# Attention heads two at a time, and the recurrence output with tokens on partitions

## The reference

```python
o_intra = jnp.einsum('bnhts,bnshv->bnthv', att, v)          # inside a chunk
o_inter = jnp.einsum('bnthk,nbhkv->bnthv', q * jnp.exp(cum), s_start)   # state at the chunk's start
o = o_f + rev(o_b)                                          # both directions
o = rms_norm(o, onorm) * jax.nn.silu(hd(zg))                # mean square over a head's 64 channels
```

```python
s_loc = jnp.einsum('bnqhgd,bnkhd->bnhgqk', qb, kb) * SCALE   # masked to the window
s_ctx = jnp.einsum('bnqhgd,blhd->bnhgql', qb, kc) * SCALE
p = jax.nn.softmax(jnp.concatenate([s_loc, s_ctx, s_sink], axis=-1), axis=-1)
o = p[..., :nk] @ v_band + p[..., nk:] @ v_cache
merged = g_a * (y_a @ wb_a) + g_b * (y_b @ wb_b) + g_c * (y_c @ wb_c) + g_d * (y_d @ wb_d)
```

## Time and profile before

| | us |
|---|---|
| median of 3 runs (1871.96 to 1878.03) | 1876.58 |
| the profiled execution | 1872.46 |
| its span | 1870.6 |
| PE busy in the span | 1696.6 |
| DVE, ACT, POOL busy | 553.6, 416.7, 222.5 |

### The profile page before, as it was taken

The page is one execution under the profiler, slowest core; times in us unless marked ns, Lnnn a source line. Parts: engine busy times, 40 slices in busy tenths (PEclk is TensorE's granted clock), DMA queues, the critical chain, the costliest instruction groups (busy, mean ns, idle before and its releaser), DMA issues. The chain is left out here.

```text
span 1870.6 us, 26968 instructions
## 1 busy us (share of the span) xinstructions
PE 1696.6 (91%) x9388; PEld 1072.3 (57%) x9388; DVE 553.6 (30%) x1317; ACT 416.7 (22%) x869; POOL 222.5 (12%) x182
## 2 busy tenths in 40 slices
PE   6989999999999897899789899999999998878887
PEld 3656556665585554555466546566557755545455
DVE  2155563321115111111132465534111241111112
ACT  3121225530103111111122012355201211111110
POOL 0003020000000232232100030100000012232220
PEclk8998899999998999999999898999999989999998
DMA  9502126533227799999982022262323179999993
GB/s 364 203 23 76 30 87 210 178 119 106 75 91 268 281 373 387 355 374 392 362 293 80 23 90 34 69 229 70 118 90 135 68 256 335 389 379 354 374 383 129
DMA packets 166115, 385.93 MB, mean 206 GB/s; under 512 B 21020, under 2 KB 58908, under 8 KB 165536
## 3 DMA queue, kind: packets, MB, share of 16 engines
q1 hardware_dynamic: 140976, 340.28, 49.1%
q0 software_dynamic: 16992, 24.96, 5.7%
q10 hardware_dynamic: 8016, 18.97, 2.7%
HBM read 372.34 MB, written 31.98 MB: 216 GB/s over the span
## 5 line engine op out<-in xcount | busy, mean ns | idle before, releaser
L756 PE MATMUL ab<-hT,slot 128*128 128x384 f32 x1344 | 457.3, 497 | 13.4 <-PEq L765 7.2
L756 PE MATMUL vb<-slot,arena 128*64 128x256 f32 x2560 | 309.0, 396 | 74.3 <-PEq L806 74.3
L756 PEld LDWEIGHTS ab<-hT,slot 128*128 128x128 f32 x1344 | 258.9, 194 | 192.4 <-issue 26.5
L756 PEld LDWEIGHTS vb<-slot,arena 128*64 128x64 f32 x2560 | 206.4, 142 | 158.9 <-issue 97.7
L756 PE MATMUL vb<-arena 64*64 64x16 f32 (+3 forms) x1272 | 152.3, 345 | 27.7 <-PEq L765 24.4
L658 POOL DMA_INDIRECT expert_sums<-arena,sum_index x72 | 112.9, 1568 | 371.7 <-POOLq L647 173.8
L1982 DVE SCALAR_TENSOR_TENSOR arena<-vb,unit_gate,arena 128x128 f32<-128x128 f32 x80 | 28.1, 351 | 411.5 <-DVEq L1981 411.5
L756 PEld LDWEIGHTS vb<-arena 64*64 64x64 f32 (+2 forms) x1272 | 84.2, 180 | 70.6 <-issue 68.0
L756 PE MATMUL ab<-slot,hT 128*128 128x384 f32 (+1 forms) x384 | 118.8, 464 | 0.0
L790 PEld LDWEIGHTS ab<-con,arena 128*128 128x128 f32 x560 | 61.3, 142 | 87.3 <-issue 86.2
L1461 ACT ACTIVATE arena<-vb 128x128 f32<-128x128 f32 x92 | 25.5, 278 | 368.0 <-ACTq L1460 368.0
(11 more groups left out here) (257 smaller groups left out, 1601.7 us busy)
## 6 DMA issues: line engine op xcount, KB each, us to landing
slot<-in_w_up SPq DMA_DIRECT2D x64, 2048.0 KB
slot<-in_w_mod SPq DMA_DIRECT2D x24, 2048.0 KB
slot<-in_w_mgate SPq DMA_DIRECT2D x32, 1024.0 KB
nat<-in_w_down SPq DMA_DIRECT2D x32, 1024.0 KB, 19.5
slot<-in_w_in SPq DMA_DIRECT2D x10, 2048.0 KB
arena<-in_w_down SPq DMA_DIRECT2D x16, 1024.0 KB, 18.9
hT<-in_w_down SPq DMA_DIRECT2D x16, 1024.0 KB, 17.1
slot<-in_w_out SPq DMA_DIRECT2D x4, 2048.0 KB
```

The costliest lines, as they stand in the source:

```text
L756: i = nc.tensor.matmul(out, lhsT, rhs, start=start, stop=stop, skip_group_check=True)
```

## The change

**The recurrence output** has tokens on partitions now. Per block, four products have all 128 rows and 128 columns (the masked scores as weights), and write each head's values twice, side by side. Then 16 products follow, one for 32 tokens (two chunks), a pair and a half: weights of 64 rows by 32 tokens, and the states of both chunks, 128 columns, streaming past. Each row of the result holds a wrong chunk's term in one of its halves; DVE takes the right half by a 0/1 column `parity` (even or odd chunk), with four operations per block in place of one. The two halves of the channels (h2 = 0, 1) go to two banks of `vb`. The norm is then per token: DVE sums squares, ACT takes 12 roots per partition, DVE inverts and scales. Six transposes on PE bring it back, standing behind the first gate product, and DVE scales and gates out of PSUM. The two `blk64` products are gone.

**Attention** takes two heads at a time, one with its operands in rows 0 to 63 and the other in rows 64 to 127. Their scores alternate and go to two banks; their value products alternate between columns 0 to 63 and 64 to 127 of one bank. The second pair's scores lie in `qkr` and `nat`, so that there are two pairs of score buffers. The filling is a plan: before the transposes of pair 0 stand unit 6, a modulation and unit 7, and then between transposes and `pv` of the five pairs what the plan lists ("8m9" is unit 8, a modulation, unit 9). The first gate product of pass 1 stands before the wait for `ya_ready`.

```diff
+PAIRS = ((0, 3), (1, 4), (2, 5), (6, 7), (8, 9))
+    plan = (("6m7", "8m9", "amb", "cmd", "mem", "mf"),
+            ("6m7", "89", "ab", "cd", "mem", "mf"))[l]
...  # PE, recurrence output
+                        banks = pair_of_banks()
+                        for pr in range(2):
+                            for h2 in range(2):
+                                h = 2 * pr + h2
+                                mm(vb[banks[h2]][:, P * pr:P * pr + P].rearrange("p (a b) -> p a b", b=HD), attS[t][:, h, :],
+                                   nat[:, t, HD * h:HD * h + HD].unsqueeze(1).to_broadcast([P, 2, HD]), pr == 0, False)
+                        for pr in range(2):
+                            for g in range(4):
+                                row = TC * t + 2 * g + (t > 0) + r
                                 for h2 in range(2):
                                     q = slice(64 * h2, 64 * h2 + 64)
...
-                                        last = mm(o[q, P * pr + CH * c:P * pr + CH * c + CH], S[q, pr, row, :],
-                                                  QX[q, pr, n0:n0 + CH], False, c == TC - 1)
+                                    last = mm(vb[banks[h2]][32 * g:32 * g + 32, P * pr:P * pr + P],
+                                              QX[q, pr, P * t + 32 * g:P * t + 32 * g + 32],
+                                              S[q, pr, row:row + 2, :].rearrange("p a b -> p (a b)"), False, True, True)
...
-                pe.wait_ge(osq_ready, 1).then_inc(osq_ready, -1)
-                for pr in range(2):
-                    group(a, lambda o: run(o[:, 0:T], [(c_("blk64"), DD[:, pr, :])]))
...
                 gate_of(PASSES[0], 0)
+                pe.wait_ge(o_normal_ready, 1).then_inc(o_normal_ready, -1)
+                for pr in range(2):
+                    group(v, lambda o: trans(o, [oN[:, t, 2 * pr:2 * pr + 2, :].rearrange("p h d -> p (h d)") for t in range(NT)]))
                 gate_of(PASSES[0], 1)
...  # PE, attention
+                        for part in range(1 if t == 0 else 2):
+                            for b, (qc, kc, cc, p0) in zip(banks, at):
+                                q = slice(p0, p0 + 64)
+                                keys = qkT[q, kc, 0:P] if t == 0 else (qkT[q, kc, P:T], kcT[q, cc, :])[part]
+                                last = mm(vb[b][:, n0:n1], qkT[q, qc, P * t:P * t + P], keys, True, True, True)
...
+                scores(0)
+                open_mod = fill(steps[0], False)
+                for j, pair in enumerate(PAIRS):
+                    if j + 1 < len(PAIRS):
+                        scores(j + 1)
+                    for m in range(2):
+                        pe.wait_ge(p_ready, 1).then_inc(p_ready, -1)
+                        group(a, lambda o: trans(o, [block_of_head(j, m, k) for k in range(4)]))
+                        group(a, lambda o: trans(o, [block_of_head(j, m, k) for k in range(4, 7)]))
+                    open_mod = fill(steps[1 + j], open_mod)
+                    pe.wait_ge(pt_ready, 2).then_inc(pt_ready, -2)
...
                 pe.drain().then_inc(attention_done, 1)
+                gate_of(PASSES[1], 0)
                 pe.wait_ge(ya_ready, 1).then_inc(ya_ready, -1)
-                for u in range(UNITS):
+                branch_of(PASSES[1], 0)
+                for u in range(1, UNITS):
                     gated(PASSES[1], u)
...  # DVE
-                vec.reciprocal(QE, QE)
...
+                vec.reduce_sum(small[:, 0:12], DD.rearrange("p a b -> p (a b)").rearrange("p (a b) -> p a b", b=HD), axis=AX.X)
...
+                scaled(0)
+                open_mod = fill(steps[0], None)
                 normalised(0)
+                for j in range(len(PAIRS)):
+                    if j + 1 < len(PAIRS):
+                        scaled(j + 1)
+                        normalised(j + 1)
+                    open_mod = fill(steps[1 + j], open_mod)
```

More of the change, by code:

```diff
@@ L158, with attention_fill @@
 NORM_MODS = [(1, 4), (1, 5)]
+def attention_fill(l):
+    plan = (("6m7", "8m9", "amb", "cmd", "mem", "mf"),
+            ("6m7", "89", "ab", "cd", "mem", "mf"))[l]
+    i, steps = 0, []
+    for part in plan:
+        step = []
+        for x in part:
+            step.append(("mod", i) if x == "m" else ("unit", int(x, 16)))
+            i += x == "m"
+        steps.append(step)
+    assert i == len(ATT_MODS[l])
+    return steps
 def slot_plan():
@@ L180, in slot_plan, with unit @@
         passing(6 + (len(START_MODS) if l == 0 else len(TAIL_MODS) + len(NORM_MODS)))
-        for p in range(2):
-            for u in range(UNITS):
[L183 to L192, removed]
+        def unit(u):
+            if u % 8 == 0:
+                take("branch")
+            if u % 4 == 0:
+                take("gate")
+            if u % 4 == 3:
+                give("gate")
+            if u % 8 == 7:
+                give("branch")
+        for u in range(EARLY_UNITS):
+            unit(u)
+        for kind, x in itertools.chain(*attention_fill(l)):
+            unit(x) if kind == "unit" else passing(1)
+        for u in range(UNITS):
+            unit(u)
         take("out0"), take("out1"), give("out0"), give("out1")
@@ L919, in _, with pair_of_banks @@
                     pe.wait_ge(states_ready, 1).then_inc(states_ready, -1)
[L920 to L927 removed]
+                    def pair_of_banks():
+                        banks = [v.next(), v.next()]
+                        for b in banks:
+                            pe.wait_ge(vfree[b], 1).then_inc(vfree[b], -1)
+                        return banks
@@ L1816, in _, with fill @@
+                def fill(step, open_mod):
+                    for kind, x in step:
+                        if kind == "unit":
+                            gated(0, x)
+                        if open_mod is not None:
+                            modulated(*ATT_MODS[l][open_mod])
+                        open_mod = x if kind == "mod" else None
+                    return open_mod
+                steps = attention_fill(l)
                 scaled(0)
+                open_mod = fill(steps[0], None)
```

303 lines of the change are left out of this document (166 added, 137 removed).

## The result

The changed kernel takes 1813.39 us (median of 4 runs, 1810.74 to 1816.84) against 1874.27 (4 runs, 1871.12 to 1878.03): a ratio of 0.9675, 95% interval 0.9645 to 0.9706, 61 us less. The forecast was 1807 with a range of 1790 to 1835. The profiled execution after took 1810.8 us, its span 1809.0, 61.6 less than the span before.

The account below looks back on a forecast made before the run. The prediction saw PE's work bounding attention and the recurrence output (there at half clock), and loads bounding the experts. Gains of 33.4 us per layer, 66.8 for two, took 1872.5 to 1805.7; it said 1807, range 1790 to 1835.

Parts of the forecast that it names:

- step 1: Recurrence output, twice per layer: fewer, longer, overlapping products cut both stages' 15.11 and 14.69 us to 8.3 each, gaining 13.2.
- step 2: Behind the recurrence output: full clock in projections and pooling, `blk64` gone, six transposes added; 4.7 us gained per layer.
- steps 3 to 6: Attention: paired scores and value products, waits that go, less one new wait; 15.5 us gained per layer.
- fourth rival: Attention's value products and the recurrence output: column places in the same rows don't overlap; 1832 us, chance 0.07.
- first rival: Recurrence output: the clock falls there all the same; 16 + 8 us more, 1831 us, chance 0.16.
- Steps 3 and 4: Attention: paired heads' scores overlap by row halves, value products by column halves; gains 7.3 and 8.0 us per layer.
- second rival: Attention's scores and the recurrence output: row halves overlap less than read; 1828 us, chance 0.08.
- Step 5: Attention: PE's waits before unit 8, the last value products and pass 1 go; 3.5 us gained per layer.
- Step 6: Attention, between first and second pair: PE waits while DVE merges units 6 and 7, then divides; 3.3 us lost per layer.
- fifth rival: Attention: the clock falls inside it; up to 220 us more, about 1890 us if partly affected, chance 0.05.
- third rival: Attention: a pair's chain is late, with 2.5 us of waiting at each of ten pairs; 1832 us, chance 0.04.

Follow-up runs that it names:

- pairs in one half: Changed kernel with two of five pairs having both heads' score operands in one row half, and value products head after head, not alternating: 1829.11 us.
- dividing first: Changed kernel with one line moved, so DVE divides the first pair before it merges units 6 and 7: 1801.84 us.
- the late drain: Changed kernel with PE's drain and the attention-done signal moved behind the first gate product of pass 1: 1815.1 us.
- the three moves: Changed kernel with DVE dividing before merging, ACT's key/value stores behind its copies, and PE's drain behind pass 1's first gate product: 1801.83 us.

## Why the prediction was right, and where it was off

The direction, the mechanism and the range hold. The sum was 66.8 us, the spans show 61.6. By stage, from the starts of the stages on PE in the two profiled executions:

| us per layer | forecast | layer 0 | layer 1 |
|---|---|---|---|
| step 1, the two output stages | 13.2 | 14.0 | 13.8 |
| step 2, stages behind them | 4.7 | 2.3 | 4.2 |
| steps 3 to 6, attention | 15.5 | 12.7 | 15.8 |
| sum | 33.4 | 29.0 | 33.8 |

To 62.8 for both come 1.2 us ahead of layer 0's output and between the layers, and 2.4 are lost again behind layer 1's attention. 1.7 of them stand in its output projection, which takes 43.17 us for 41.49: behind a gap of 2.08 us, in both kernels, the clock was 0.85 and 0.94 in its first windows of 8 us, where it was 1.00 before.

**Step 1** held, with its size a little low. I priced the products with the states at 1.0 us per block by the modulation product's overlap of 3.6. The row shows 0.59 us; 32 records of 0.109 us are 3.49, so 5.9 ran at once. Row halves and column places overlap together. Three blocks at 1.0 less 0.59 are 1.2 us; the products inside the chunks, 1.05 to 1.09 us per block for the 0.87 in the sum, took back 0.6. The lead was right, 2.77 us (135.30 to 138.07) for 2.7.

The Trainium skill, "TensorE: Matmul & The Clock Gate", Part 3 (Packing small matmuls), says that a weight load overlaps running products only where the row group differs. The prediction took this one sentence to mean that only two of the states' products would work at once. The trace does not bear out that reading, with 5.9 at once among the states' products and with value products of 1.68 us per pair that use all rows in both heads. The fourth rival, which was the time by that reading, falls with it. Row halves do count for the scores, as the 1.39 against 0.76 us of pairs in one half show.

**Step 2**: the three terms came in (projections 1.75 for 1.86, pooling products 1.29 for 1.39, `blk64` gone), with no wait before the transposes. What failed in layer 0 is "if the clock stays up". It stayed up in the output, but fell later, behind a gap of 2.14 us that was there before too: 3.30 for 1.94 us at 181.27. That is not the new output's doing alone: with the pairs alone, and so with the old output, the next 8 records fell too, 3.53 us behind 2.20. The wait at 171.83 grew from 1.34 to 1.78, since PE is there 9.1 us earlier and what it waits for comes only 8.6 us earlier. In layer 1 the fall was smaller (2.84 us for the same 8 records) and the waits before and after it were shorter (1.09 and 1.46 us), hence 4.2. The first rival falls, and the short products show on which side of it the change stands: with 16 columns per product the clock goes.

**Steps 3 and 4** were sized well. A pair's scores take 2.13 us for 2.0 (gain 6.65 instead of 7.3), its value products 1.68 for 1.75 (8.3 instead of 8.0). The second rival is out; pairs in one half show what it would have looked like.

**Step 5**: the three waits went, 1.17, 1.11 and 1.25 us, but a new one took the place of the third, 1.21 us in layer 0 and 0.57 in layer 1. Before, it was the last copy, as I had read it: that ended at 403.82, PE went on at 404.45, and the gate's weights had been asked for 28.6 us ahead, with a DMA share of 0.01 from 384 to 386.

```profile
375.85 1.55 SPq L533 DMA_DIRECT2D slot<-in_w_mgate  x2
```

In the new order of slots the same weights are asked for only 9.4 us ahead, at 365.80. What failed is the sentence that a slot free one unit (6.6 us) before its weights are used is early enough: over both layers of the changed kernel, of dividing first, of the late drain and of the three moves, PE goes on 8.8 to 9.7 us behind the issue of this load.

**Step 6** is the step with the largest miss. The wait came where it was put and nowhere else: 0.70 + 3.19 us in layer 0 and 0.70 + 2.88 in layer 1, for 3.3. But it let the clock fall, and the scores (0.7), transposes (1.45) and gate product (0.65) behind it lost another 2.8 us in layer 0. In layer 1 it was 2.35. This was the mechanism of the fifth rival, at a small part of its price: 5 us in all, not 70. The third rival, waits at every pair, is out: there is one.

On the other side stands a fall that I had not seen in the kernel before. I read one window of 4 us in the middle of attention and wrote that the clock is 1.00. Over all of attention it was 0.97, because of its start:

```profile
270.24 1.58 PE L756 MATMUL vb<-arena 64*128 64x128 f32 x4 [1.51 <-PEq L765]
...
273.46 7.22 PE L756 MATMUL ab<-hT,slot 128*128 128x384 f32 x16
```

The first scores and gate product took 3.22 and 7.05 us for 1.7 and 5.2, and 3.12 and 7.16 in layer 1. After the change this fall is smaller in layer 0 (3.23 us for a pair's scores, 2.10 without it, the gate product at full clock) and absent in layer 1, which gives 2.2 and 3.4 us that no step counted. All traces together show what goes with it. With heads one at a time (before, recurrence alone) and with pairs in one half the gate product there took 6.4 to 7.9 us, in both layers. In the seven kernels with alternating pairs the clock fell there in 2 of 14 cases. So this gain goes with alternating pairs, but to the forecast it was luck: without it some 56 us would have been gained and not 61.6.

## What to carry to other kernels

Small products on part of the array gain twice when they are turned so that they stream more columns and alternate between places: they overlap (5.9 at once here), and the clock holds behind them. When a chain is refilled, look at what stands idle just before the first new wait: here DVE idled 7.45 us ahead of work that it could have done first, and one moved line gave back 11.5 us. Price a wait of PE with the work behind it at half clock, and read the clock over the whole stage, not in one window of it.

## What the runs showed of the hardware

- The clock fell with PE busy in all of a window: 2.00 of 2.00 us with 88 records of 16 columns at 1.00, then 0.65, then 0.50. Busy time alone doesn't hold it up.
- Behind a gap of PE of some 2 us the clock falls in one execution and not in the next. The same 8 records behind a gap of 2.14 us took 3.30 us in the changed kernel, 3.31 with the recurrence output alone, 3.57 with the division first, and 1.94 in the kernel before and with the three moves together, where the next 8 records fell (3.31 behind 2.29). What decides it is open; each such fall costs 1 to 3 us. It is part of why executions of one program differ: in the profile with the division first PE is 5.2 us behind the changed kernel at 45.79, where both still run the same program, with a mean clock of 0.58 from 18 to 46 for 0.70.
- A product cut into short pieces pays by the piece. At half clock 256 records of 16 columns on 64 rows and 32 columns took 11.03 us, 43 ns each, and in the window at 1.00 some 88 of them went in 2.00 us, 23 ns each. At full clock 32 records of 128 columns, eight times as long, took 0.59 us, 18 ns each. The 8.25 us of the first block are a mix of both clocks.
